# The identity of a delta-rule solve's first level, moved from VectorE to GpSimd, one tile behind another

## The chip, the cores and the metric

The kernel runs on one core of a Trainium2 chip, as one program of 69,816 instructions. The metric is the device time of one execution in microseconds (us). Five engines work side by side, each through its own list of instructions in order: TensorE (PE), VectorE (DVE), ScalarE (ACT), GpSimd (POOL) and SyncE (SP, which here starts transfers). They wait for each other through semaphores.

## The reference, cut to what matters

The reference is one inference step of a decoder layer: two feed-forward blocks, attention, and an RWKV-7 time mixing whose core is a delta-rule recurrence over a matrix state of each head:

```python
def step(S, inp):
    rt, wt, kt, vt, at, bt = inp
    sa = jnp.einsum("bhvk,bhk->bhv", S, at)
    S = S * wt[:, :, None, :] + sa[..., None] * bt[:, :, None, :] + vt[..., None] * kt[:, :, None, :]
    return S, jnp.einsum("bhvk,bhk->bhv", S, rt)
```

There are 8 heads of 64, a prompt of 1024 tokens and 8 samples of 4 tokens (32 tokens). All is float32. Only the stage that computes this recurrence is changed.

## The kernel before

The stage is `rwkv_phase` (L2106 to L2800), and it lies between about 2050 and 2550 us of the span. The recurrence is cut into chunks of 32 tokens (4 for the samples). Inside a chunk the dependence of each token on the earlier ones is a triangular system, which is solved by doubling: the inverse of 2x2 blocks first, then `LEVELS` = 4 levels, each of which joins blocks of twice the size.

**Tiles and groups.** A tile is 128 tokens of one pair of heads. There are 9 tiles for each of 4 pairs of heads: 8 of prompt and one of samples. Three tiles make a group i (0 to 11), which is tiles 3i to 3i+2. The third tile of groups 2, 5, 8 and 11 is the sample tile, and its expansions are 8 chunks wide where the others are 4. The text calls groups by what the group after them is: the elementwise work "ahead" is done for group i+1 while group i is solved, and it is 384 tokens wide, but 288 where group i+1 holds the samples (i = 1, 4, 7, 10).

**One written-out order.** A list `jobs` (L2224 to L2229) fixes the order of all work. Every engine walks the same list and does its own part of each job, in that order. For each group the list has:
- `start_of(i)`: for the three tiles `turn` (four transposes, copied out by ACT), `products` for two halves (PE; DVE masks the results into `prod` and `xx`, L2603 and L2605), `seed` (adds the identity to `xx`, L2527), then for each level `off` (PE; DVE out L2608) and `grow` (PE; DVE out L2613), then `nv` and `gh`;
- merged evenly into it, `chain_of(i-1)`: the recurrence from chunk to chunk of the group before (`chain`, PE L2786, DVE out L2636; `y`, L2663 and L2645);
- merged evenly into that, `spread_of(i)` (POOL) and `beside`, which is `ahead_of(i+1)` and `after_of(i-2)`;
- at the end `rest_of(i)`: `rgy`, `trans`, `add`.

**Jobs that matter here.** `spread` is the job "expansions": POOL builds `b_exp` and `k_exp` (L2402) and `decay` (L2410) of one tile. They are needed by `trans` and `add` at the end of the group. `mix_k` (DVE: difference L2515, mix L2518, scale L2538), `mix_r` (L2515, L2518) and `mix_v` (POOL: difference L2373; DVE: mix L2518) form the inputs of group i+1. `scan` is a prefix sum on DVE (L2542), after which POOL does two subtractions (L2360, L2363). `w`, `a` and `g` (L2675, L2677, L2679) and `norm`, `rksum`, `mean`, `var` (all L2693) are single wide products of PE. PE's results go through 7 PSUM banks in turn: a job may start when the job 7 places earlier in PE's list has been read out.

**Waits of the seed.** `off` of level 0 waits for `seeded` (L2720). `mix_v` on DVE waits for POOL's difference through `v_diffed` (L2516).

Of the kernel before, what the change touches and what calls it, by code (L numbers as in the profile page):

```python
# [10 lines left out]
ALU = mybir.AluOpType  # L11
# [3 lines left out]
P = 128  # L15
# [2090 lines left out]
def rwkv_phase(nc, env, masks, lw, lg, proj, shift, params, lora_w, not_start, state_in, yb_dram,  # L2106
# [10 lines left out]
    LEVELS, GT, BANKS, HB = 4, 3, 7, P // 2  # L2117
# [5 lines left out]
    with Phase(nc) as ctx:  # L2123
        def sb(n, shape):
            return ctx.enter_context(nc.sbuf_tensor(f"rw_{n}", shape, F32))

        def sem(n):
            return ctx.enter_context(nc.semaphore(f"rw_{n}"))
# [14 lines left out]
        xx = sb("xx", [P, GT, 4, HB])  # L2143
# [12 lines left out]
        expanded, seeded, decayed, rg_done = (sem(n) for n in ("expanded", "seeded", "decayed", "rg_done"))  # L2156
# [12 lines left out]
        strict4, level_mask, chunk_mask, seeds, ident_half = masks  # L2169

        def halves(t):
            return 1 if t % NTILE == NTILE - 1 else 2
# [7 lines left out]
        def tiles_of(i):  # L2180
            return range(i * GT, (i + 1) * GT)

        def start_of(i):
            g = tiles_of(i)
            first = [("turn", t, 0) for t in g]
            first += [("products", t, h) for t in g for h in range(2)]
            first += [("seed", t, 0) for t in g]
            for lv in range(LEVELS):
                first += [("off", t, lv) for t in g] + [("grow", t, lv) for t in g]
            return first + [("nv", t, 0) for t in g] + [("gh", t, 0) for t in g]  # L2190

        def rest_of(i):
            g = tiles_of(i)
            rest = [("rgy", t, a) for t in g for a in range(halves(t))]
            return rest + [("trans", t, 0) for t in g] + [("add", t, 0) for t in g]
# [18 lines left out]
        def spread_of(i):  # L2214
            return [("spread", t, 0) for t in tiles_of(i)]

        def merged(x, more):

            out = []
            for n, item in enumerate(x):  # L2220
                out += [item] + more[n * len(more) // len(x):(n + 1) * len(more) // len(x)]
            return out

        jobs = ahead_of(0)  # L2224
        for i in range(NI):
            beside = merged(ahead_of(i + 1), after_of(i - 2)) if i + 1 < NI else after_of(i - 2)
            now = merged(start_of(i), chain_of(i - 1)) if i else start_of(i)
            jobs += merged(now, spread_of(i) + beside) + rest_of(i)
        jobs += merged(chain_of(NI - 1), after_of(NI - 2)) + after_of(NI - 1)  # L2229

        NO_PE = ("mix_k", "scan", "sq", "mix_r", "exp", "mix_v", "root", "kp", "kt", "ar_r", "kn", "ar_a", "ysq",
# [15 lines left out]
        def wait_out(eng, job):  # L2247

            eng.wait_ge(out_by[job], emptied[job])
# [4 lines left out]
        def own(t):  # L2254
            return t % GT
# [89 lines left out]
        @block.gpsimd  # L2345
        def _(pool):
            pool.memset(padded[:, 0, :, 0:1], 0.0).then_inc(zeroed, 1)
            pool.memset(ar[:, GT - 1, GT - 1, :, T_DEC:], 0.0).then_inc(zeroed, 1)
            for x in (bt, kt, bh, kh, v):
                pool.memset(x[:, GT - 1, SAMPLE + T_DEC:], 0.0).then_inc(zeroed, 1)  # L2350
            pool.memset(s_none[:, :], 0.0).then_inc(zeroed, 1)
            pool.memset(seeds[:, 0, :], 0.0).then_inc(zeroed, 1)
            pool.wait_ge(zeroed, 9)
            pool.tensor_copy(seeds[:, 0, 0:HB:2], ident_half[:, 1:HB:2]).then_inc(zeroed, 1)
            for kind, i, _ in jobs:
                if kind == "scan":
                    _, g, w, _ = place(i)
                    pool.wait_ge(scanned, i + 1)
                    wait(pool, bh_done, i)
                    pool.tensor_tensor(sg[:, 0:w], cum[:, 0:w], sg[:, 0:w], ALU.subtract)  # L2360
                    for lo, hi, c in [(0, GC, CHUNK)] if g < GT - 1 else [(0, SAMPLE, CHUNK), (SAMPLE, w, DEC_SEQ)]:
                        x = cum[:, lo:hi].rearrange("p (n t) -> p n t", t=c)
                        ins = pool.tensor_tensor(to_end[:, lo:hi].rearrange("p (n t) -> p n t", t=c),  # L2363
                                                 x[:, :, c - 1:c].broadcast_to([P, (hi - lo) // c, c]), x,
                                                 ALU.subtract)
                    ins.then_inc(ended, 1)
                elif kind == "mix_v":
                    p, g, _, _ = place(i)
                    pool.wait_ge(loaded[g], LOADS[g] * (p + 1))
                    if i >= GT:  # L2370
                        wait_out(pool, ("rksum", i - GT, 0))
                    for cur, prev, out in pieces(g, 2, v[:, g, :]):
                        pool.tensor_tensor(out, prev, cur, ALU.subtract).then_inc(v_diffed, 1)  # L2373
                elif kind == "kt":
                    _, g, w, _ = place(i)
                    pool.wait_ge(kp_done, i + 1)
                    pool.wait_ge(exped, i + 1)
                    pool.tensor_tensor(kh[:, g, 0:w], k[:, 0:w], to_end[:, 0:w], ALU.mult).then_inc(kh_done, 1)
                elif kind == "ar_a":
                    _, g, w, _ = place(i)  # L2380
                    pool.wait_ge(bb_done, i + 1)
                    pool.tensor_tensor(bh[:, g, 0:w], a_in[:, 0:w], to_end[:, 0:w], ALU.mult).then_inc(bh_done, 1)
                elif kind == "ygate":
                    p, _, w, _ = place(i)
                    x = y[:, i % 2, 0:w]
                    pool.wait_ge(y_scaled, i + 1)
                    pool.tensor_scalar(x, x, par[:, p, PAR_LNW:PAR_LNW + 1], par[:, p, PAR_LNB:PAR_LNB + 1],
                                       ALU.mult, ALU.add).then_inc(affine, 1)
                    pool.wait_ge(affine, i + 1)
                    wait_out(pool, ("rksum", i, 0))  # L2390
                    pool.tensor_tensor(x, x, bonus[:, i % 4, 0:w], ALU.add).then_inc(with_bonus, 1)
                    pool.wait_ge(with_bonus, i + 1)
                    wait_out(pool, ("g", i, 0))
                    pool.tensor_tensor(x, x, g_out[:, i % 4, 0:w], ALU.mult).then_inc(gated, 1)
                elif kind == "spread":
                    t, o, n = i, own(i), chunks(i)
                    wait_out(pool, ("turn", t, 0))
                    if t >= GT:
                        wait_done(pool, ("add", t - GT, 0))
                    m = chunk_mask(t)  # L2400
                    for dst, col in ((b_exp, 2), (k_exp, 3)):
                        pool.tensor_tensor(dst[:, 4 * o:4 * o + n, :],  # L2402
                                           tok[:, o, col:col + 1, :].broadcast_to([P, n, P]),
                                           m.rearrange("p (n a) -> p n a", a=1).broadcast_to([P, n, P]),
                                           ALU.mult).then_inc(expanded, 1)
                    if t >= GT:
                        wait_out(pool, ("trans", t - GT, 0))
                    pool.wait_ge(exped, t // GT + 1)
                    c0 = 4 * o
                    pool.tensor_tensor(decay[:, 4 * o:4 * o + n, :],  # L2410
                                       ident_half.rearrange("p (a n) -> p a n", a=1).broadcast_to([P, n, 64]),
                                       e_c[:, slot(t), c0:c0 + n].rearrange("p (n a) -> p n a", a=1)
                                       .broadcast_to([P, n, 64]), ALU.mult).then_inc(decayed, 1)
# [92 lines left out]
        def _(dve):  # L2506
# [14 lines left out]
            for job in jobs:  # L2521
                kind, i, a = job
                if kind == "seed":

                    o = own(i)
                    wait_out(dve, ("products", i, 1))
                    dve.tensor_tensor(xx[:, o, :, :], xx[:, o, :, :],  # L2527
                                      ident_half.rearrange("p (a n) -> p a n", a=1).broadcast_to([P, 4, HB]),
                                      ALU.add).then_inc(seeded, 1)
                    continue  # L2530
                if kind in NO_PE:
                    p, g, w, cols = place(i)
# [48 lines left out]
                if kind in ("norm", "rksum", "mean"):  # L2581
                    _, g, w, _ = place(i)
# [14 lines left out]
                t, o, lt = i, own(i), i % NTILE  # L2597
                i = t // GT
# [22 lines left out]
                elif kind == "trans":  # L2621
                    n = chunks(t)
# [400 lines left out]
```

## Time and profile before

| | |
|---|---|
| median of 3 runs | 3797.13 us (3793.44 to 3805.70) |
| the profiled execution, its own time | 3798.92 us |
| its span in the profile | 3797.1 us |
| its mean granted TensorE clock | 0.944 of full speed |
| busy over the span: PE, DVE, ACT, POOL | 90%, 44%, 25%, 11% |
| from 2090 to 2540 us: PE, DVE, ACT, POOL busy | 386.8, 333.8, 160.8, 185.9 us of 450 |

A row of a timeline gives start and length in us, engine, line, operation, what is written and read, and how often in a row; in brackets stands the idle time of the engine before it, and what ended it. The ends of matmuls are modelled and overlap, so on PE the distance between starts says more than the length. DVE and POOL instructions overlap their neighbours by some hundredths too.

### The profile page before, as it was taken

Reading aid. Unit: us, or ns where it says so; the run is one execution under the profiler, and the core shown is the slowest. Engines: PE = TensorE matmul, PEld = TensorE weight load, DVE = VectorE, ACT = ScalarE, POOL = GpSimd, SP = SyncE. Lnnn points to the kernel's source line nnn. Section 1 sums busy time; section 2 is a strip of 40 time slices with the busy share of each in tenths; the row PEclk is TensorE's granted clock in tenths of the full one; section 3 lists DMA queues with packets and bytes.
Section 4 is the critical chain, followed back from the end, with each engine's and each line's share of the span. In section 5 each row is a group of like instructions: output and inputs, shape, how many; then the busy total and the mean of one; then the engine's idle time right before and its main releaser. Section 6 shows DMA issues by size and latency. Waiting matters only on the chain. (4 is left out here: it accounts for less than half of the span.)

```text
span 3797.1 us, 69816 instructions
## 1 busy us (share of the span) xinstructions
PE 3436.2 (90%) x29021; PEld 3071.1 (81%) x29021; DVE 1678.9 (44%) x2939; ACT 935.5 (25%) x1619; POOL 428.2 (11%) x452
## 2 busy tenths in 40 slices
PE   7999999979999799979994888878979999999877
PEld 6999999978999646756663676768969999999866
DVE  3343343353222245435443777755243344344454
ACT  3111111121001104534442333324241111111231
POOL 0000000020000000033331444430010000000112
PEclk9999999989999898989996899989989999999988
DMA  2111111123222300056553010004131011011032
GB/s 104 35 55 45 40 50 45 40 78 115 90 90 90 123 2 13 9 190 206 195 201 86 14 32 25 16 32 175 35 130 50 35 52 49 34 52 47 24 139 99
DMA packets 118587, 279.27 MB, mean 74 GB/s; under 512 B 45876, under 2 KB 56948, under 8 KB 117780
## 3 DMA queue, kind: packets, MB, share of 16 engines
q1 hardware_dynamic: 99892, 199.87, 15.7%
q0 software_dynamic: 18432, 75.51, 5.8%
q8 instruction: 212, 3.47, 0.4%
q14 instruction: 51, 0.42, 0.0%
HBM read 231.41 MB, written 43.80 MB: 72 GB/s over the span
## 5 line engine op out<-in xcount | busy, mean ns | idle before, releaser
L79 PE MATMUL f_psg<-f_u_hi,f_w_hi 128*128 128x352 f32 x1056 | 348.7, 330 | 46.1 <-DVE f_u_lo L359 23.0
L590 DVE TENSOR_TENSOR c_x<-c_x,f_psd 128x352 f32<-128x352 f32 x480 | 246.2, 519 | 317.0 <-PE f_psd L81 317.0
L79 PE MATMUL f_psd<-f_hid_hi,f_w_hi 128*128 128x352 f32 x1056 | 349.8, 331 | 18.2 <-DVE c_x L590 9.8
L475 ACT ACTIVATE f_w_hi<-f_raw 128x1024 fp32r<-128x1024 f32 x132 | 136.8, 1054 | 912.6 <-PE f_psd L81 352.0
L80 PE MATMUL f_psg<-f_u_lo,f_w_hi 128*128 128x352 f32 x1056 | 343.5, 325 | 0.0
L81 PE MATMUL f_psg<-f_u_hi,f_w_lo 128*128 128x352 f32 x1056 | 343.4, 325 | 0.0
L79 PE MATMUL f_psu<-f_u_hi,f_w_hi 128*128 128x352 f32 x1056 | 341.6, 323 | 0.4 <-DVE f_w_lo L479 0.4
L80 PE MATMUL f_psd<-f_hid_lo,f_w_hi 128*128 128x352 f32 x1056 | 341.3, 323 | 0.0
L81 PE MATMUL f_psd<-f_hid_hi,f_w_lo 128*128 128x352 f32 x1056 | 340.9, 323 | 0.0
L80 PE MATMUL f_psu<-f_u_lo,f_w_hi 128*128 128x352 f32 x1056 | 339.1, 321 | 0.0
L81 PE MATMUL f_psu<-f_u_hi,f_w_lo 128*128 128x352 f32 x1056 | 338.7, 321 | 0.0
L479 DVE TENSOR_TENSOR f_w_lo<-f_raw,f_w_hi 128x1024 fp32r<-128x1024 f32 x132 | 161.6, 1238 | 361.2 <-ACT f_w_hi L475 361.2
L79 PE MATMUL in_ps<-in_u_hi,inw_hi 128*128 128x352 f32 x864 | 284.3, 329 | 12.3 <-DVE in_u_lo L359 8.9
L81 PE MATMUL in_ps<-in_u_hi,inw_lo 128*128 128x352 f32 x864 | 282.0, 326 | 0.0
L80 PE MATMUL in_ps<-in_u_lo,inw_hi 128*128 128x352 f32 x864 | 280.5, 325 | 0.0
L79 PEld LDWEIGHTS f_psg<-f_u_hi,f_w_hi 128*128 128x128 f32 x1056 | 202.4, 192 | 58.2 <-DVE f_u_lo L359 30.0
L118 POOL TENSOR_TENSOR n_total<-n_total,n_sq 128x1056 f32<-128x1056 f32 x18 | 44.5, 2470 | 1687.4 <-ACT n_sq L111 1687.4
L79 PEld LDWEIGHTS f_psd<-f_hid_hi,f_w_hi 128*128 128x128 f32 x1056 | 199.3, 189 | 35.0 <-DVE c_x L590 20.2
L80 PEld LDWEIGHTS f_psg<-f_u_lo,f_w_hi 128*128 128x128 f32 x1056 | 202.9, 192 | 0.0
L81 PEld LDWEIGHTS f_psg<-f_u_hi,f_w_lo 128*128 128x128 f32 x1056 | 202.2, 192 | 0.0
L80 PEld LDWEIGHTS f_psd<-f_hid_lo,f_w_hi 128*128 128x128 f32 x1056 | 199.7, 189 | 0.0
L81 PEld LDWEIGHTS f_psd<-f_hid_hi,f_w_lo 128*128 128x128 f32 x1056 | 199.6, 189 | 0.0
(403 smaller groups left out, 7178.6 us busy)
## 6 DMA issues: line engine op xcount, KB each, us to landing
f_raw<-in_ffn_gu SPq DMA_DIRECT2D x88, 512.0 KB, 4.2
f_raw<-in_ffn_d SPq DMA_DIRECT2D x44, 512.0 KB, 3.8
proj<-in_out SPq DMA_DIRECT2D x36, 528.0 KB, 2.9
inw_raw<-in_w_in_units SPq DMA_DIRECT2D x36, 512.0 KB, 3.9
h<-c_x SPq DMA_DIRECT2D x24, 528.0 KB, 2.9
c_x<-proj SPq DMA_DIRECT2D x16, 528.0 KB, 4.3
mgw_raw<-in_merge_units SPq DMA_DIRECT2D x16, 512.0 KB, 4.6
plw_raw<-in_ple_units SPq DMA_DIRECT2D x8, 640.0 KB, 3.9
```

The source lines that it names most:

```text
L79: pe.matmul(out, w_hi, x_hi, start=start, stop=False)
L80: pe.matmul(out, w_hi, x_lo, start=False, stop=False)
L81: return pe.matmul(out, w_lo, x_hi, start=False, stop=stop)
L118: eng.tensor_tensor(total, total, self.buf.sq[:, c % 2, :], ALU.add).then_inc(self.added, 1)
L475: act.activation(w_hi[:, u % 3, :], raw[:, u % 3, :], ACT.Copy).then_inc(hi_done, 1)
L479: dve.tensor_tensor(w_lo[:, u % 3, :], raw[:, u % 3, :], w_hi[:, u % 3, :], ALU.subtract).then_inc(lo_done, 1)
L590: dve.tensor_tensor(a, a, ps_d[:, n % 2, 0:TB], ALU.add).then_inc(added, 1)
```

## The change

The identity is added by POOL, and the list of jobs is put in another order. The three `seed` jobs no longer follow all six `products` jobs: each stands behind its own tile's. The three `spread` jobs, which were merged in at the front of the group, now follow the third `seed` in `start_of(i)`, and are no longer in the list that is merged in beside. As the lists are merged by their lengths, the jobs of `beside` also shift against those of `start_of` and `chain_of`.

```diff
             first = [("turn", t, 0) for t in g]
-            first += [("products", t, h) for t in g for h in range(2)]
-            first += [("seed", t, 0) for t in g]
+            for t in g:
+                first += [("products", t, 0), ("products", t, 1), ("seed", t, 0)]
+            first += spread_of(i)
...
-            jobs += merged(now, spread_of(i) + beside) + rest_of(i)
+            jobs += merged(now, beside) + rest_of(i)
...
+                elif kind == "seed":
+                    o = own(i)
+                    wait_out(pool, ("products", i, 1))
+                    pool.tensor_tensor(xx[:, o, :, :], xx[:, o, :, :],
+                                       ident_half.rearrange("p (a n) -> p a n", a=1).broadcast_to([P, 4, HB]),
+                                       ALU.add).then_inc(seeded, 1)
...
                 if kind == "seed":
-
-                    o = own(i)
-                    wait_out(dve, ("products", i, 1))
-                    dve.tensor_tensor(xx[:, o, :, :], xx[:, o, :, :],
-                                      ident_half.rearrange("p (a n) -> p a n", a=1).broadcast_to([P, 4, HB]),
-                                      ALU.add).then_inc(seeded, 1)
                     continue
```

For group 5 the list up to `mix_v` reads as follows (capitals: jobs of `beside`; a number after a dot is a half, a level or a chunk).

Before: turn15 turn16 turn17 **spread15** chain12.0 products15.0 **spread16** products15.1 products16.0 **spread17** chain12.1 products16.1 W products17.0 products17.1 A chain12.2 **seed15 seed16** MIX_K **seed17** chain12.3 MEAN off15.0 off16.0 SCAN y12 off17.0 G grow15.0 grow16.0 SQ chain13.0 grow17.0 off15.1 YSQ off16.1 chain13.1 MIX_R off17.1 grow15.1 NORM grow16.1 chain13.2 EXP grow17.1 off15.2 VAR off16.2 chain13.3 off17.2 MIX_V

After: turn15 turn16 turn17 W chain12.0 products15.0 products15.1 A **seed15** chain12.1 MIX_K products16.0 products16.1 **seed16** MEAN chain12.2 products17.0 products17.1 SCAN **seed17** chain12.3 G **spread15 spread16 spread17** SQ y12 off15.0 YSQ off16.0 off17.0 chain13.0 MIX_R grow15.0 grow16.0 grow17.0 NORM chain13.1 off15.1 EXP off16.1 off17.1 chain13.2 VAR grow15.1 grow16.1 MIX_V grow17.1 chain13.3 off15.2 ROOT off16.2 off17.2

## Rows read from the trace of the kernel before

**Rows 1.** Who waited for whom, 2090 to 2540 us: total, times, longest.
```profile
PE rw_ps L2725 <- DVE rw_s L2636: 15.2, 8, 2.6
PE rw_ps L2725 <- DVE rw_xx L2527: 14.4, 16, 2.4
```

**Rows 2.** Groups of DVE instructions, 2090 to 2540 us: busy us, mean ns, idle before.
```profile
L2527 DVE TENSOR_TENSOR rw_xx<-rw_xx,c_ident_half 128x256 f32<-128x256 f32 x36 | 36.6, 1048 | 0.0
...
L2542 DVE TENSOR_TENSOR_SCAN rw_cum<-rw_starts,rw_sg 128x384 f32<-128x384 f32 x7 | 6.6, 945 | 0.0
...
L2518 DVE SCALAR_TENSOR_TENSOR rw_r<-rw_r,rw_par,rw_padded 128x384 f32<-128x384 f32 x7 | 4.3, 619 | 0.2
...
L2515 DVE TENSOR_TENSOR rw_r<-rw_padded 128x384 f32<-128x384 f32 x7 | 3.8, 547 | 0.0
L2538 DVE TENSOR_SCALAR rw_kk<-rw_k,rw_par 128x384 f32<-128x384 f32 x7 | 2.9, 420 | 0.2
```

**Rows 3.** Timeline of POOL, group 5 (its third tile's expansions).
```profile
2280.35 1.90 POOL L2402 TENSOR_TENSOR rw_b_exp<-rw_tok,c_in_chunk 128x1024 f32<-128x1024 f32 x1
...
2284.24 1.22 POOL L2410 TENSOR_TENSOR rw_decay<-c_ident_half,rw_e_c 128x512 f32<-128x512 f32 x1
```

**Rows 4.** Timeline of DVE, group 5.
```profile
2279.18 0.43 DVE L2603 TENSOR_TENSOR rw_prod<-rw_ps,c_strict 128x256 f32<-128x256 f32 x1 [0.48 <-PE rw_ps L2716]
...
2279.71 0.41 DVE L2603 TENSOR_TENSOR rw_prod<-rw_ps,c_strict 128x256 f32<-128x256 f32 x1
...
2280.59 3.96 DVE L2527 TENSOR_TENSOR rw_xx<-rw_xx,c_ident_half 128x256 f32<-128x256 f32 x2
2284.48 1.39 DVE L2515 TENSOR_TENSOR rw_k<-rw_padded 128x384 f32<-128x384 f32 x1
...
2298.07 0.61 DVE L2518 SCALAR_TENSOR_TENSOR rw_v<-rw_v,rw_par,rw_padded 128x384 f32<-128x384 f32 x1
```

**Rows 5.** Timeline of PE, group 5: first transpose, chain12.0, w, off17.0, off17.2.
```profile
2273.85 0.33 PE L2706 MATMUL rw_ps<-c_ident,rw_ar 128*128 128x128 f32 x1
...
2275.31 0.33 PE L2786 MATMUL rw_ps<-rw_s,rw_trans 64*64 64x64 f32 x4
...
2277.52 0.91 PE L2675 MATMUL rw_ps<-c_lw,rw_lora 64*128 64x384 f32 x2
...
2287.47 0.69 PE L2725 MATMUL rw_ps<-rw_xx,rw_prod 64*64 64x64 f32 x8 [1.91 <-DVE rw_s L2636]
...
2297.42 0.40 PE L2725 MATMUL rw_ps<-rw_xx,rw_prod 64*64 64x64 f32 x8
```

**Rows 6.** Busy us by stretch: PE, PEld, DVE, ACT, POOL, then PEclk, DMA, GB/s.
```profile
2284.00:2292.00 8.00, 5.39 (x74) 4.12 (x76) 6.22 (x14) 2.21 (x4) 4.03 (x5) 0.57 0.00 0
```

**Rows 7.** Groups of POOL instructions, 2090 to 2540 us.
```profile
L2402 POOL TENSOR_TENSOR rw_k_exp<-rw_tok,c_in_chunk 128x512 f32<-128x512 f32 x32 | 34.7, 1084 | 0.0
...
L2410 POOL TENSOR_TENSOR rw_decay<-c_ident_half,rw_e_c 128x256 f32<-128x256 f32 x32 | 21.4, 669 | 0.0
...
L2360 POOL TENSOR_TENSOR rw_sg<-rw_cum,rw_sg 128x384 f32<-128x384 f32 x7 | 7.0, 994 | 24.2 <-DVE rw_cum L2542 24.2
...
L2363 POOL TENSOR_TENSOR rw_to_end<-rw_cum 128x384 f32<-128x384 f32 x7 | 5.8, 825 | 0.0
L2373 POOL TENSOR_TENSOR rw_v<-rw_padded 128x384 f32<-128x384 f32 x7 | 5.8, 824 | 0.0
```

**Rows 8.** Timelines, groups 4 and 6: first transpose, and DVE's part of mix_v.
```profile
2238.81 0.33 PE L2706 MATMUL rw_ps<-c_ident,rw_ar 128*128 128x128 f32 x1
...
2259.98 0.64 DVE L2518 SCALAR_TENSOR_TENSOR rw_v<-rw_v,rw_par,rw_padded 128x256 f32<-128x256 f32 x2
...
2314.52 0.33 PE L2706 MATMUL rw_ps<-c_ident,rw_ar 128*128 128x128 f32 x1
...
2335.95 0.61 DVE L2518 SCALAR_TENSOR_TENSOR rw_v<-rw_v,rw_par,rw_padded 128x384 f32<-128x384 f32 x1
```

**Rows 9.** Timeline of DVE, group 11: its three seeds.
```profile
2508.28 4.93 DVE L2527 TENSOR_TENSOR rw_xx<-rw_xx,c_ident_half 128x256 f32<-128x256 f32 x3
```

## The prediction

> **What bounds the kernel now.** I read the page first: the change touches one stage, about 450 of 3797 us, in which PE is busy 387 us and DVE 334 us. So neither engine is idle for long, and what counts is where each group of three tiles loses time. The list of waits names the place [rows 1]: at `off` of level 0 PE waited 14.4 us for seeds and 15.2 us for a copy of `chain` that stands behind the seeds on DVE. The two together, 29.6 us over 12 groups, are what could be won directly. The groups of DVE instructions say why the seeds are late [rows 2]: 36 of them take 36.6 us, 1048 ns each, although they are no larger than the masking of the products, which takes 0.41 us [rows 4]. The timelines of group 5 show what stretches them. The two seeds at 2280.59 last 3.96 us, about 2 us each, just while POOL does the expansions of the sample tile from 2280.35 [rows 3, 4]. The difference of `mix_k` behind them takes 1.39 us [rows 4] where the same difference for `mix_r`, with POOL idle, takes 0.55 us [rows 2]. The masking of the products, which reads one side from PSUM, ran at 0.41 to 0.43 us beside POOL's work too [rows 4]. PE then stands still (1.91 us before off17.0 alone [rows 5]), and its granted clock falls: 0.57 as a mean from 2284 to 2292, which is mostly the lower of its two levels, 1.2 GHz [rows 6].
>
> The Trainium skill, "SBUF — State Buffer", section "Who interferes with whom", has a rule for this: a DVE instruction with two SBUF inputs and a GpSimd instruction that reads SBUF lock each other out for a whole instruction. By that rule a seed behind a 2 us expansion lasts 2 us, which is what the trace shows (3.96 us for two). The same rule speaks against the change as well: seeds on GpSimd can be held up by DVE's two-input instructions, here `mix_k` and `scan`, by up to the 0.5 to 0.95 us that these last.
>
> **The change part by part.** Times are from the group's first transpose (T). I follow the two lists of the text above, for a group with 384 columns ahead.
>
> *Removed from DVE:* three seeds, 3 x 1.05 = 3.1 us a group [rows 2], and the stretching of `mix_k`, about 0.8 us (1.39 against 0.55). In group 5 that is nearly the whole hole of PE before off17.0.
>
> *The seed on POOL:* the trace has no such instruction. The nearest rows are `decay`, the same 256 columns, two inputs, at 669 ns, and the 384 column differences at 824 to 994 ns [rows 7]. From below it can't be under DVE's unstretched 0.41, and from above 0.99. I take 0.65, from the row of equal size.
>
> *The order on POOL, which is the heart of it.* The list of after puts `scan` in front of the third seed. POOL goes through it in order, so the third seed waits for DVE's scan and then for POOL's own two subtractions. When is the scan done?
> - The turns end at T+1.46 (2273.85 to 2275.31). Six jobs of chain and products followed in 2.21 us, so 0.37 each [rows 5]. After has turns, w, chain, 2 products, a, chain: 1.46 + 2 x 0.91 + 4 x 0.37 = T+4.8.
> - DVE copies that chain (0.2), does `mix_k` unstretched (0.55 + 0.62 + 0.42 = 1.6 [rows 2]), two products (0.53 apart, from 2279.18 and 2279.71 [rows 4], 1.06), the mean (about 0.5, the size of the 384 column rows), a chain (0.15), two products (1.06) and the scan (0.95): T+10.3.
> - POOL: 0.99 + 0.83 [rows 7], then the seed 0.65: T+12.7. Without the scan ahead of it the third seed would be done at about T+10.0.
>
> So off of the third tile starts at T+12.8. Before it started at T+13.6 in group 5 (2287.47), with `g` still to come. PE gains there, some 2 to 3 us in group 5 and under 1 us where no sample tile stretched the seeds.
>
> *The expansions.* They follow the third seed, where before they followed the turns (T+1.5). Three tiles take 3 x (2 x 1.08 + 0.67) = 8.5 us by the mean rows [rows 7], less some overlap, 8.3; with a sample tile two of 2.65 and one of 5.1 (2280.35 to 2284.24 + 1.22 [rows 3]), with 0.4 for DVE in between 10.8. They end at T+21.0 and T+23.5. Their own users, `trans` and `add`, come later than that, so that is hidden. But behind them on POOL stands the difference of `mix_v`, 0.83 [rows 7], and DVE waits for it **at a place that the new list has moved forward**: before grow17.1, not behind off17.2. DVE's mix ends 0.6 later:
> - 384 ahead, no samples: T+22.4. Before it ended at 2336.5, T+22.0 [rows 8], and with four more copies done, which I put at 0.2 each, so after stands at 23.2: **1.3 us later**.
> - 288 ahead: the narrower w, a, mix_k, scan and subtractions bring the third seed 0.9 us forward, T+11.8, expansions to 20.1, differences and mix 1.4: T+21.5, with a grow, a chain and three offs to copy, 1.1: 22.6. Before: 2260.6, T+21.8 [rows 8]. **0.85 later**.
> - With the sample tile: 23.5 + 0.83 + 0.6 = T+24.9, with 1.1: 26.0. Before: 2298.7, T+24.8 [rows 4, 5]. **1.25 later**.
>
> What waits behind: DVE's copy of the third grow of level 1, and through it the third off of level 2, on which PE stops once it has done the few jobs ahead of it. PE's own lag, by the same sum in group 5, is off17.2 at 24.9 + 0.35 = T+25.3 against 2297.42, T+23.6: 1.7 us [rows 5]. From there on DVE is nearly always busy until the end of the group, so what is late there stays late.
>
> *The last group* has nothing ahead, so neither the scan nor mix_v. Its seeds take DVE 4.93 us before [rows 9]; on POOL the third follows its products within 0.7, so about 3.5 us are won.
>
> *The granted clock.* DVE arrives at mix_v at about T+20.5 and stands there 1 to 4 us, longest with the sample tile. A hole of that size before off17.0 dropped PE's clock to the lower level [rows 5, 6]. I add 1 us for each of three groups; the bounds are nothing and the 3 us or so that PE's 5.39 us of work in such a stretch [rows 6] lost.
>
> *The sum:* 4 x 1.3 + 4 x 0.85 + 3 x 1.25 = 12.4, less 3.5, plus 3: **+12 us**. By PE's lag in place of DVE's it is 11 x 1.7 - 3.5 + 3 = +18; with the seed at its bounds (-0.25, +0.35) 11 groups give -3 and +4. The profiled execution took 3798.9 us, 1.8 over the median; applied to the median of 3797.1 it gives **3809 us**.
>
> **The rivals.**
> - *POOL is done in time, and the win stays.* If POOL is through the expansions before DVE gets to mix_v, the stall goes, and what counts is the earlier end of level 0. In group 5, with PE at its full clock, I make that about 3 us; 0.7 us in the eight others; 3.5 in the last group: 3 x 3 + 8 x 0.7 + 3.5 = -18 us, 3779. It decides if the difference of `mix_v` is out by about T+20.5, and by my sum it is out at 21.8. For it speaks the size of the waits [rows 1]; against it, that 8.3 us of POOL work have moved by some 11 us. A partial form, the expansions 1 us earlier than my sum in each group, ends at about 0.
> - *The two cancel.* The early gain is kept as slack that PE uses up while DVE waits: PE has four or five jobs of 0.3 to 0.45 us to do before it needs the missing copy, and its idle places later in the group soak up 1 us of the lag. Then 11 x 0.3 + 3 - 3.5, within 5 us of before.
> - *The stall costs more.* PE's clock falls at each stall, and `mix_r` (two instructions with both inputs in SBUF), now beside the expansions, is stretched as `mix_k` was, by 0.8 us: 11 x (1.7 + 0.8) + 3 = +30 us, 3827.
> - *The third seed itself is the new hole*, 2.3 us of idle PE before off17.0. It is in my sum, but hidden under the later stall. Alone it ends near before.
>
> **How the numbers follow.** About 0.3% (11 us) is what a measurement of this kernel can tell from no change. My forecast (+4 to +20) has 0.45, costs more 0.1, cancel 0.25, the win stays (with its partial forms) 0.2. Half or more of my own case lies above 11 us: slower 0.45 of it and the dear case together come to 0.48, the same 0.3, faster 0.22. The range leaves out the outer parts of the first and third rival: 3784 to 3825.
>
> **What would show it.** Right: no wait of PE for the seeds of the first two tiles; DVE's seeds gone and the difference of mix_k at 0.55 us; POOL's third seed directly behind L2363; a wait of DVE at L2518 for POOL's `rw_v` L2373 of 1 to 4 us in most groups, which before had almost none; a PE wait for `rw_xx` L2613 behind it. Wrong: if that wait is absent, the first rival has it; if it is there and the stage is no longer than before, the second. Most of all I could be wrong in the 1 us by which two sums of twelve terms differ.

## The result and the profile after

The changed kernel takes 3820.69 us (median of 6 runs, 3815.61 to 3825.72), the one before 3804.34 us in the same session (6 runs, 3793.44 to 3806.25). The medians are 16.4 us apart. The ratio that is used here and below isn't that of the medians: it is 1.0049, with a 95% interval of 1.0038 to 1.0060, which makes the changed kernel slower by 19 us (14 to 23). The prediction was +12 us. The profiled execution took 3817.18 us, with a span of 3815.4 us and a mean granted clock of 0.944, as before.

First, who waited for whom in the changed kernel, 2090 to 2570 us (total us, times, longest). It answers to [rows 1].

```profile
PE rw_ps L2726 <- POOL rw_xx L2399: 24.3, 12, 4.9
PE rw_ps L2787 <- DVE rw_s L2637: 22.0, 22, 2.6
...
DVE rw_v L2525 <- POOL rw_v L2374: 10.3, 6, 3.0
PE rw_ps L2726 <- DVE rw_s L2637: 10.3, 6, 3.5
```

PE's wait for DVE's seeds is gone and a longer one for POOL's third seed stands in its place: 24.3 us against 14.4. DVE's wait for `rw_v`, which the prediction was built on, is there, but in 6 groups of 11, and only in four of them (0, 2, 5 and 8) for 1 us or more. The second row is new too: at `chain` PE waits 22.0 us for DVE's copies, where in the kernel before it waited 12.1 (2090 to 2540 us):

```profile
PE rw_ps L2786 <- DVE rw_s L2636: 12.1, 15, 2.3
```

Next the groups of instructions that answer to [rows 2] (busy us, mean ns, idle before).

```profile
L2399 POOL TENSOR_TENSOR rw_xx<-rw_xx,c_ident_half 128x256 f32<-128x256 f32 x36 | 26.9, 746 | 118.2 <-DVE rw_xx L2606 117.3 <-PE rw_ps L2726 0.9
...
L2522 DVE TENSOR_TENSOR rw_r<-rw_padded 128x384 f32<-128x384 f32 x7 | 7.4, 1064 | 0.0
L2525 DVE SCALAR_TENSOR_TENSOR rw_r<-rw_r,rw_par,rw_padded 128x384 f32<-128x384 f32 x7 | 7.2, 1033 | 0.2
L2522 DVE TENSOR_TENSOR rw_k<-rw_padded 128x384 f32<-128x384 f32 x7 | 5.7, 820 | 0.0
```

`mix_r` takes 1064 + 1033 ns where before it took 547 + 619 [rows 2]: it now lies beside the expansions. The timeline of POOL in group 5 (T = 2288.45) shows the order in which they come.

```profile
2296.43 0.72 POOL L2399 TENSOR_TENSOR rw_xx<-rw_xx,c_ident_half 128x256 f32<-128x256 f32 x1 [2.67 <-DVE rw_xx L2606]
2298.94 1.00 POOL L2361 TENSOR_TENSOR rw_sg<-rw_cum,rw_sg 128x384 f32<-128x384 f32 x1 [1.79 <-DVE rw_cum L2543]
2299.90 0.82 POOL L2364 TENSOR_TENSOR rw_to_end<-rw_cum 128x384 f32<-128x384 f32 x1
2300.68 0.72 POOL L2399 TENSOR_TENSOR rw_xx<-rw_xx,c_ident_half 128x256 f32<-128x256 f32 x1
2301.36 1.04 POOL L2409 TENSOR_TENSOR rw_b_exp<-rw_tok,c_in_chunk 128x512 f32<-128x512 f32 x1
...
2310.84 1.04 POOL L2417 TENSOR_TENSOR rw_decay<-c_ident_half,rw_e_c 128x512 f32<-128x512 f32 x1
2311.84 0.82 POOL L2374 TENSOR_TENSOR rw_v<-rw_padded 128x384 f32<-128x384 f32 x1
```

The third seed stands behind the scan's two subtractions and ends at 2301.40, T+12.95. The difference of `mix_v` stands behind all expansions and ends at T+24.2. What PE and DVE do about it in the same group:

```profile
2301.55 0.69 PE L2726 MATMUL rw_ps<-rw_xx,rw_prod 64*64 64x64 f32 x8 [2.56 <-POOL rw_xx L2399]
...
2313.86 0.69 PE L2726 MATMUL rw_ps<-rw_xx,rw_prod 64*64 64x64 f32 x8 [2.87 <-DVE rw_s L2637]
```

```profile
2302.63 1.18 DVE L2522 TENSOR_TENSOR rw_r<-rw_padded 128x384 f32<-128x384 f32 x1
2303.85 0.85 DVE L2525 SCALAR_TENSOR_TENSOR rw_r<-rw_r,rw_par,rw_padded 128x384 f32<-128x384 f32 x1
...
2312.77 0.62 DVE L2525 SCALAR_TENSOR_TENSOR rw_v<-rw_v,rw_par,rw_padded 128x384 f32<-128x384 f32 x1 [2.37 <-POOL rw_v L2374]
```

PE stands still twice, 2.56 us for the third seed and 2.87 us for off17.2, where before the longest of the group was 1.91 us [rows 5]. The clock is at the lower level when PE resumes after the first (0.50 from 2300 us on) and falls again after the second (busy us of PE, PEld, DVE, ACT, POOL, then PEclk, DMA share, GB/s):

```profile
2302.00:2305.00 3.00, 3.00 (x61) 3.00 (x58) 2.69 (x6) 0.80 (x2) 3.00 (x4) 0.50 0.00 0
2312.00:2317.00 5.00, 3.14 (x63) 3.17 (x65) 3.61 (x11) 0.00 (x0) 1.57 (x2) 0.66 0.02 3
```

From 2302 to 2305 PE works without a pause at 0.50, the 1.2 GHz level. The same view for the whole of group 5, in the kernel before and in the changed one:

```profile
2273.85:2314.52 40.67, 33.64 (x711) 27.18 (x707) 30.75 (x82) 14.26 (x33) 18.13 (x17) 0.92 0.16 25
2288.45:2331.32 42.87, 34.49 (x711) 28.21 (x707) 26.99 (x79) 14.21 (x33) 20.49 (x20) 0.88 0.16 26
```

PE does the same number of matmul instructions in both, 711, but is busy 0.85 us longer, at a mean clock of 0.88 instead of 0.92.

In the groups with 288 columns ahead DVE hardly waits for `rw_v`. Group 4 (T = 2251.83), timeline of DVE:

```profile
2265.28 1.56 DVE L2522 TENSOR_TENSOR rw_r<-rw_padded 128x256 f32<-128x256 f32 x2
2266.88 2.14 DVE L2525 SCALAR_TENSOR_TENSOR rw_r<-rw_r,rw_par,rw_padded 128x256 f32<-128x256 f32 x2
...
2273.23 0.64 DVE L2525 SCALAR_TENSOR_TENSOR rw_v<-rw_v,rw_par,rw_padded 128x256 f32<-128x256 f32 x2
```

`mix_r` takes 3.70 us there (1.56 + 2.14), and DVE comes to `mix_v` only when POOL's difference is ready. In the kernel before the same two rows are:

```profile
2255.47 0.51 DVE L2515 TENSOR_TENSOR rw_r<-rw_padded 128x256 f32<-128x256 f32 x2
2256.02 0.65 DVE L2518 SCALAR_TENSOR_TENSOR rw_r<-rw_r,rw_par,rw_padded 128x256 f32<-128x256 f32 x2
```

**Where the time went.** From first transpose to first transpose, groups 0 to 10 took 412.4 us before and 431.5 after: +19.1. By kind: +4.8 over the four plain groups (0, 3, 6, 9), +7.7 over the four with 288 columns ahead, +6.5 over the three with the sample tile. From the last group's first transpose (2502.32 and 2525.78) to the stage's last POOL instruction (its end at 2554.95 and 2573.57) it is 52.6 and 47.8: -4.8. So the stage is 14.2 us longer. The first transposes are another 4.4 us apart, in code that the change doesn't touch, and that is within chance: in the traces of the ten experiments, whose code up to there is the same, the first transpose lies between 2088.07 and 2100.03 us. Of the 19.1 us, PE stands idle for 15.5 and is busy 3.6 longer (355.4 and 359.0 us).

### The profile page after: what moved, and what is told of

It reads as the page before. It is cut to its first block and busy times, and to the rows that moved or that the text cites. A ratio compares the mean times of both kernels' runs of the same rounds, so it can differ in the third digit from the quotient of the medians.

```text
span 3815.4 us, 69816 instructions
## 1 busy us (share of the span) xinstructions
PE 3437.9 (90%) x29021; PEld 3070.7 (80%) x29021; DVE 1656.7 (43%) x2903; ACT 935.1 (25%) x1619; POOL 453.8 (12%) x488
## 5 line engine op out<-in xcount | busy, mean ns | idle before, releaser
L79 PEld LDWEIGHTS f_psu<-f_u_hi,f_w_hi 128*128 128x128 f32 x1056 | 199.2, 189 | 0.8 <-DVE f_w_lo L479 0.8
```

Of the source, the lines that this page charges most:

```text
L79: pe.matmul(out, w_hi, x_hi, start=start, stop=False)
```

## The experiments

Each was run beside the kernel before, whose median was 3799.6, 3800.7 and 3800.3 us in the three sessions; "back" is against the changed kernel's 1.0049. The 95% interval stands behind each ratio; it is 3 to 7 us to either side, so differences of 1 to 3 us between versions are not resolved. Most alter only the order in which one engine walks the list. POOL then walks `order` in place of `jobs`, and DVE, ACT and PE keep theirs:

```python
order = list(jobs)
def behind(job, at):
    if job in order and order.index(job) < order.index(at):
        order.remove(job)
        order.insert(order.index(at) + 1, job)
def ahead(job, at):
    if job in order and order.index(job) > order.index(at):
        order.remove(job)
        order.insert(order.index(at), job)
```

It adds 14 to 17 lines, so L2399 of the changed kernel is L2413 to L2416 there.

**Scan's subtractions behind the third seed**

```diff
+            for n in range(NI):
+                behind(("scan", n + 1, 0), ("seed", n * GT + 2, 0))
```

> POOL alone walks the changed list with its two subtractions of the scan behind the third seed instead of ahead of it. Theory (the wait of DVE at mix_v for POOL's difference decides, as in the prediction): the third seed comes about 2 us sooner, but the difference of mix_v is as late as before, so most of what is won at the seed is given back there: at most 8 us of the 19 us come back, 3812 to 3819 on the scale where before is 3804. Rival (the hole before the third off of level 0 decides; the list of waits of the changed kernel has 24.3 us there and only 10.3 us at mix_v): 15 to 22 us come back, at or under the time of before, 3798 to 3806.

3819.44 us, ratio 1.0047 (1.0031 to 1.0064): 1 us back, which is nothing. Its waits:

```profile
DVE rw_v L2539 <- POOL rw_v L2388: 28.9, 11, 5.1
PE rw_ps L2740 <- DVE rw_s L2651: 25.1, 6, 5.6
...
PE rw_ps L2740 <- POOL rw_xx L2413: 6.8, 9, 2.9
```

PE's wait for POOL's seeds falls from 24.3 to 6.8 us, and DVE's for `rw_v` grows from 10.3 to 28.9. The early seed was won and paid back at `mix_v`: while POOL's difference is late, the third seed is hidden under it.

**POOL's difference of mix_v ahead of the expansions**

```diff
+                ahead(("mix_v", n + 1, 0), ("spread", n * GT, 0))
```

> POOL alone walks the changed list with the difference of mix_v ahead of the three expansions instead of behind them. Theory (mix_v decides): the 10.3 us of DVE waits go, and PE's waits and low clock behind them: 10 to 18 us come back, 3803 to 3811 where before is 3804. Rival (the third seed decides): under 6 us come back, 3815 or more.

3805.07 us, ratio 1.0014 (1.0001 to 1.0027): 13 us back of 19. DVE no longer waits for `rw_v`; in group 5 its mix ends at T+21.8 (2306.50 against 2284.74). By kind of group, in its trace, the three sample groups win 9.3 us (119.1 against 128.4), the four plain ones 2.6, and the four with 288 columns ahead only 0.8 (145.7 against 146.5, and 138.8 in the kernel before). The wait for the third seed is untouched:

```profile
PE rw_ps L2740 <- POOL rw_xx L2413: 25.4, 13, 4.9
```

**Both moves.** The two lines of the two runs above together.

> Both moves on POOL: third seed, two subtractions, difference of mix_v, then the expansions. If the two waits hide each other, as the prediction has it, the two together give more than the sum of the single ones, and the kernel is faster than before by what the prediction's first rival worked out: 3780 to 3794 where before is 3804. If the loss sits in the order of the jobs on PE and DVE and not in POOL's order, it stays at 3810 or more.

3793.68 us, ratio 0.9987 (0.9974 to 1.0000): 24 us back, where the two alone gave 1 and 13. So with `mix_v` out of the way the third seed is worth another 11 us. That is 5 us faster than before, where 10 to 24 were expected. In its trace the 288-column groups are now back at 139.2 us, so what they had lost came back only with the third seed. What may hold the rest back is in its groups of instructions:

```profile
L2569 DVE SCALAR_TENSOR_TENSOR rw_k<-rw_gate,rw_k 128x384 f32<-128x384 f32 x7 | 9.2, 1316 | 0.2
L2540 DVE SCALAR_TENSOR_TENSOR rw_r<-rw_r,rw_par,rw_padded 128x384 f32<-128x384 f32 x7 | 8.3, 1186 | 0.2
```

`rw_k<-rw_gate` took 559 ns in the kernel before, where no expansion lay beside it. The expansions have been moved onto other steps of DVE.

**The new order alone, seeds on DVE.** 

```diff
-                elif kind == "seed":
...
                 if kind == "seed":
+                    o = own(i)
+                    wait_out(dve, ("products", i, 1))
+                    dve.tensor_tensor(xx[:, o, :, :], xx[:, o, :, :],
...
```

> The changed list, with the seeds left on DVE: the order without the change of engine. The seeds then take DVE 3 x 0.35 us a group and do not wait behind the scan's two subtractions on POOL. Theory (mix_v decides): the expansions start where they did in the changed kernel less 0.7 us, mix_v is still late, 3812 to 3820. Rival (the third seed decides): 3798 to 3808.

3814.64 us, ratio 1.0048 (1.0031 to 1.0066): the whole loss, a little above the 8 to 16 us expected, without any seed on POOL. The seeds are no longer stretched on DVE (451 ns against 1048), and it doesn't help:

```profile
L2527 DVE TENSOR_TENSOR rw_xx<-rw_xx,c_ident_half 128x256 f32<-128x256 f32 x36 | 16.2, 451 | 0.7
...
DVE rw_v L2519 <- POOL rw_v L2374: 25.4, 11, 5.1
```

**The engine alone, old order.** 

```diff
-            for t in g:
-                first += [("products", t, 0), ("products", t, 1), ("seed", t, 0)]
-            first += spread_of(i)
+            first += [("products", t, h) for t in g for h in range(2)]
+            first += [("seed", t, 0) for t in g]
...
-            jobs += merged(now, beside) + rest_of(i)
+            jobs += merged(now, spread_of(i) + beside) + rest_of(i)
```

> The list of before, seeds on POOL: the change of engine without the new order. On POOL the seeds stand behind the three expansions. By the rows of before these end 8.4 us after the first transpose (11.6 with a sample tile), and the seeds follow, 0.7 us each. Theory: PE waits for them about as long as it waited for the stretched seeds of before, mix_k on DVE is still stretched, and mix_v is not touched: within 8 us of before, 3793 to 3809 where before is 3800. Rival (the engine is what costs): slower by 12 us or more.

3809.59 us, ratio 1.0023 (1.0012 to 1.0034): 9 us slower than before, just outside the 8 of the theory and below the 12 of the rival. What the trace shows is not what costs in the changed kernel: POOL now has the expansions ahead of all three seeds, and DVE's `mix_k` lies beside their end (waits, and groups):

```profile
PE rw_ps L2725 <- POOL rw_xx L2398: 41.8, 19, 4.7
```

```profile
L2524 DVE SCALAR_TENSOR_TENSOR rw_k<-rw_k,rw_par,rw_padded 128x384 f32<-128x384 f32 x7 | 10.9, 1551 | 0.2
L2521 DVE TENSOR_TENSOR rw_k<-rw_padded 128x384 f32<-128x384 f32 x7 | 8.9, 1275 | 0.0
L2538 DVE TENSOR_SCALAR rw_kk<-rw_k,rw_par 128x384 f32<-128x384 f32 x7 | 6.9, 986 | 0.2
```

**The kernel before, POOL's expansions behind its difference of mix_v.** DVE does the seeds and the list is the old one; POOL alone walks it in another order.

```diff
+            for n in range(NI):
+                for t in reversed(range(n * GT, n * GT + GT)):
+                    behind(("spread", t, 0), ("mix_v", n + 1, 0) if n + 1 < NI else ("seed", n * GT + 2, 0))
```

> The list of before on all engines, seeds on DVE; POOL alone does the three expansions behind the difference of mix_v. Theory: seeds (1.05 us) and mix_k's difference (1.3) fall to 0.45 and 0.55 us, nothing waits for POOL, the collision moves to later DVE instructions with two SBUF inputs, where it costs a part: 3786 to 3796 where before is 3800. Rival (stretched seeds are hidden anyway): within 3 us of before.

3796.89 us, ratio 0.9991 (0.9982 to 1.0000), about 3 us won and less than expected. Against the kernel before, the seeds fall from 1048 to 524 ns, which frees DVE of 19.0 us (36.6 - 17.6). `rw_k<-rw_gate` rises to 1460 ns, `rw_rk` to 1067, `rw_gate` to 1141 and the mix of `mix_r` to 1277:

```profile
L2542 DVE TENSOR_TENSOR rw_xx<-rw_xx,c_ident_half 128x256 f32<-128x256 f32 x36 | 17.6, 524 | 0.0
...
L2568 DVE SCALAR_TENSOR_TENSOR rw_k<-rw_gate,rw_k 128x384 f32<-128x384 f32 x7 | 10.2, 1460 | 0.2
...
L2565 DVE TENSOR_SCALAR rw_gate<-rw_a_in,rw_par 128x384 f32<-128x384 f32 x7 | 8.0, 1141 | 0.0
```

**Both moves, seeds on DVE.** The two lines of both moves and the edit that puts the addition back in DVE's part.

> As e3_both (changed list, POOL: two subtractions, difference of mix_v, then expansions), but with the seeds on DVE. It tells what the engine is worth once the order on POOL is mended: POOL's seed is 0.73 us and leaves DVE 0.35 us free. Theory (engine hardly matters): within 4 us of e3_both. Rival (DVE bound): 8 us slower than e3_both or more.

3798.18 us, ratio 0.9995 (0.9984 to 1.0005). With the seeds on POOL it was 0.9987, 3 us less, and the two intervals overlap: with this order on POOL, the engine of the seeds makes no difference that these runs can tell.

**Both moves, and the first tile's expansions ahead of the first seed**

```diff
+                ahead(("spread", n * GT, 0), ("seed", n * GT, 0))
```

> As e3_both, with the first tile's expansions ahead of the first seed on POOL, in the 3 us in which POOL stood idle. The other two then end 2.6 us sooner, and kp on DVE (1.32 us instead of 0.56 in e3_both) is stretched less. If the collisions are what is left, 3 to 8 us faster than e3_both; if the first seed is now late, no gain or a loss.

3782.44 us (5 runs, 3779.43 to 3785.92), ratio 0.9957 (0.9944 to 0.9971): 16 us faster than before, 11 faster than both moves alone (3 to 8 were expected), and the fastest of all. In the changed kernel POOL stood idle for 7.03 us ahead of the first seed of group 5; here it does one tile's expansions there (T = 2271.76):

```profile
2273.13 1.04 POOL L2425 TENSOR_TENSOR rw_b_exp<-rw_tok,c_in_chunk 128x512 f32<-128x512 f32 x1 [3.81 <-ACT rw_tok L2526]
2274.12 1.04 POOL L2425 TENSOR_TENSOR rw_k_exp<-rw_tok,c_in_chunk 128x512 f32<-128x512 f32 x1
2275.12 0.61 POOL L2433 TENSOR_TENSOR rw_decay<-c_ident_half,rw_e_c 128x256 f32<-128x256 f32 x1
2276.34 0.73 POOL L2415 TENSOR_TENSOR rw_xx<-rw_xx,c_ident_half 128x256 f32<-128x256 f32 x1 [0.60 <-DVE rw_xx L2622]
```

The seed isn't delayed (it still waits for DVE). DVE is idle until 2274.44 and then copies a chain and masks products out of PSUM, which isn't stretched (0.42 and 0.28 us). `rw_k<-rw_gate` is back at 559 ns. But POOL is also done with the group's expansions 3 us sooner (T+21.7 in group 5, T+24.7 with both moves alone), and no run tells how much of the 11 us is due to either.

**DVE's part of mix_v back at its old place.** The changed kernel; only DVE's walk of the list differs.

```diff
-            for job in jobs:
+            order = list(jobs)
+            for n in range(NI - 1):
+                late, at = ("mix_v", n + 1, 0), ("off", n * GT + 2, 2)
+                if order.index(late) < order.index(at):
+                    order.remove(late)
+                    order.insert(order.index(at) + 1, late)
+            for job in order:
```

> The changed kernel, but DVE alone does its part of mix_v where the kernel before has it, behind the eviction of the third tile's second level; POOL's order is untouched (third seed, third expansions, then its difference for mix_v). Theory (what costs is that DVE's step is brought forward past the point where POOL's difference is ready): no waits of DVE for rw_v from POOL, 8 to 14 us of the changed kernel's 19 us come back, like putting POOL's difference first did; the wait of PE for the third seed (24 us in 12 places) stays. 1.5 to 3 us slower per 1000 less: ratio to before 1.001 to 1.003. Rival (DVE's place does not matter, the stretches of DVE's steps beside POOL or the third seed's wait make the whole loss): ratio stays at 1.004 to 1.006.

3815.27 us, ratio 1.0041 (1.0028 to 1.0055): the rival holds. (Its profiled execution, 3804.69 us, was its quickest, so its trace serves for the order of things and not for lengths.) DVE's wait shrinks to 4.0 us, but `rw_v` is no sooner done:

```profile
2303.13 0.62 DVE L2525 SCALAR_TENSOR_TENSOR rw_v<-rw_v,rw_par,rw_padded 128x384 f32<-128x384 f32 x1 [0.80 <-POOL rw_v L2374]
```

The mix ends at T+24.9 (2303.75 against 2278.81), as in the changed kernel. What costs here is when POOL's difference is ready, not where DVE asks for it.

**The second tile's expansions early as well**

```diff
+                ahead(("spread", n * GT + 1, 0), ("seed", n * GT + 1, 0))
```

> The version with both POOL moves and the first tile's expansions ahead of the first seed, and now the second tile's expansions ahead of the second seed as well, in POOL's pause of about 2.7 us between the seeds. Theory (POOL's expansions cost only where DVE's shared steps lie beside them or where a seed comes late): if they fit the pause, 0 to 8 us faster than without it (ratio to before 0.9935 to 0.9957). Rival (they delay the second seed or stretch DVE's mix_k in front of it, and PE waits for the second tile): slower than without it by 3 to 12 us (ratio 0.9965 to 0.999).

3803.56 us, ratio 0.9999 (0.9986 to 1.0012): by the ratios 16 us slower than with one tile early, more than the 3 to 12 of the rival. (Its profiled execution, 3810.00 us, was its slowest.) POOL's pause between the first two seeds was 2.66 us long, and DVE's `mix_k` lies in it. Timeline of DVE, then of POOL, group 5 (T = 2284.70):

```profile
2290.46 1.28 DVE L2542 SCALAR_TENSOR_TENSOR rw_k<-rw_k,rw_par,rw_padded 128x384 f32<-128x384 f32 x1
2291.78 1.08 DVE L2556 TENSOR_SCALAR rw_kk<-rw_k,rw_par 128x384 f32<-128x384 f32 x1
```

```profile
2292.60 0.72 POOL L2434 TENSOR_TENSOR rw_decay<-c_ident_half,rw_e_c 128x256 f32<-128x256 f32 x1
2293.99 0.72 POOL L2416 TENSOR_TENSOR rw_xx<-rw_xx,c_ident_half 128x256 f32<-128x256 f32 x1 [0.67 <-DVE rw_xx L2623]
```

Two steps of `mix_k` took 2.36 us instead of 1.04 (0.62 + 0.42, as with one tile early), the copy of a chain and the second tile's products behind them came late, and PE's waits at `chain` for DVE's copies rose from 21.2 to 35.0 us (22 places).

## Why the prediction was right, and where its sizes were off

The sign, the cause and 12 of 19 us came out; four terms of the sum were off. In the traces the stage is 14.2 us longer, against a sum of 11.9, and part of that closeness is luck: 4.3 us too little for the 288-column groups stand against 0.4, 0.25 and 1.3 too much for the others. The prediction's second sum, by PE's lag of 1.7 us a group, has 18.7 for the 11 groups, which measured 19.1; it added the clock to that once more.

- **The order on POOL.** Right almost to the tenth in the sample groups. In group 5 the third seed ends at T+12.95 (12.7 predicted), POOL's difference of `mix_v` at T+24.2 and DVE's mix at T+24.9 (24.9), off17.2 starts at T+25.4 (25.3). In groups 3, 6 and 9 the seed and the difference are 0.7 us later than predicted (T+13.4 and T+22.5, for 12.7 and 21.8). DVE comes to `mix_v` at T+21.95 in group 5, not at T+20.5, so its wait is 2.4 us. That the lateness of `mix_v` is the larger part of the loss is shown: moving POOL's difference alone gave 13 us back, moving the seed alone nothing, both 24. By kind of group that holds for the sample groups, where it gave 9.3 us back, and not for the 288-column ones.
- **"At a place that the new list has moved forward"** was the half of the argument that did not matter. With the place moved back, the loss stayed within the interval.
- **"The third seed itself is the new hole"**, called hidden under the later stall: shown by the first three experiments. PE's wait for it is the longest of the stage's new waits (24.3 us), yet it is worth 1 us while `mix_v` is late, and 11 once it isn't. In the traces its gain falls in the 288-column groups (145.7 to 139.2 us) and in the plain ones (153.9 to 147.6), not in the sample groups (119.1 to 120.1). The list of waits alone would have named the wrong one.
- **Mis-sized: the 288-column groups.** 4 x 0.85 = 3.4 us were put down, 7.7 measured. DVE's `mix_v` ended at T+22.0 and not T+21.5, and in groups 4, 7 and 10 for another reason than forecast: there is no wait for POOL left, as `mix_r` beside the expansions takes 3.70 us instead of 1.16 and DVE comes late. The stretching of `mix_r` had been left to the rival "the stall costs more", at 0.8; in 384-column groups it measured 0.93 (1064 + 1033 - 547 - 619 ns), in group 4 2.5. That mechanism belonged into the sum. So did the third seed's hole, 2.3 us of PE in groups 4 and 7, which moving `mix_v` alone left as it was, with 6.9 of the 7.7 us. The clock isn't separated from the two: from the kernel before to the changed one its mean fell from 0.95 to 0.91 in groups 4, 7 and 10, but rose from 0.90 to 0.95 in group 1, which lost as much (2.2 us). The stretching may also be why a wait of 1 to 4 us for `rw_v`, forecast for most groups, was found in four: in group 4, read above, DVE was held up before it got there.
- **Mis-sized, plain groups.** 4 x 1.3 = 5.2 predicted, 4.8 measured, but by two errors: three groups lost 1.5 to 2.4 us, and group 9 became 0.9 shorter, because it had been 2.5 us longer than its like in the kernel before (39.9 against 37.5 and 37.4 for groups 3 and 6). There its mean clock was 0.87, that of the two others 0.95, and PE was busy 35.4 us against 33.0 and 32.9 with the same jobs, so the clock made group 9 longer there; why it was low isn't shown.
- **Sample groups:** 3.75 and 3 for the clock, 6.75 in all, against 6.5 measured. The two low stretches of group 5 agree with it. With the same instructions PE is busy 3.3 us longer over the three groups (104.2 against 100.9) and idle 3.2 longer, so by these rows, whose ends of matmuls are modelled, about half of the 6.5 is the clock, as forecast.
- **The last group:** -3.5 predicted, -4.8 measured; with the new order and the seeds left on DVE it is -4.3 (48.3 us), so it is mostly the order that wins it and not the engine.
- **What would show it.** No wait of PE for the first two tiles' seeds: one of 0.44 us is left, in group 0. The wait of PE behind DVE's stall was named as one for `rw_xx`; that has 4.0 us, and the larger part, 10.3 us, is put down to the copy of a chain (`rw_s`) that stands behind the same step.
- **Small prices.** The seed on POOL took 0.75 us where 0.65 was taken from the row of equal size, inside its bounds. "The difference of `mix_k` at 0.55 us" failed: 0.82, as POOL's first seed starts beside it. What that cost isn't shown.

The sum of the dear rival, +30, leaves out the 3.5 us of the last group that the other sums take off; with them it is +27.

Two things stay open: how the ratio's 19 us (14 to 23) and the 14.2 of the two traces go together, and the part played by the other jobs of the merged list, which shifted too. PE's waits at `chain` for DVE's copies are a sign of it: 12.1 us before, 22.0 in the changed kernel, and still 21.3 to 21.5 with POOL's difference moved and with both moves, but 5.6 with the old list and the seeds on POOL. In the run with the old place of `mix_v`, DVE does `rw_gate` and `rw_k` ahead of the copies of the second level; the kernel before has them behind. No run isolates that.

The Trainium skill, "SBUF — State Buffer", section "Who interferes with whom", says that the engine that issues second is shut out for the whole of the other's instruction, and counts among what can collide not only two-input instructions but also a `tensor_scalar` with its quick two-port form. The traces agree on both: 1551 against 619 ns for a two-input mix and 986 against 420 ns for the scale of `mix_k`, in the run with the engine alone changed. That the scale runs in its quick form fits its 420 ns, where a two-input difference of the same 384 columns takes 547.

## What to carry to other kernels

An engine that takes over a short step takes it at its own place in its own queue: work out for each job behind it when it now comes out, and look for the user with the earliest need, not for the longest wait. In these runs the expansions on GpSimd stretched the VectorE steps with their inputs in SBUF beside them, wherever they were put. Moving them won most where GpSimd was idle and VectorE idle too or reading PSUM, as ahead of the first seed (-11 us for one tile, and +16 for a second one in a pause that looked long enough). Where two waits lie one behind the other, undo each alone and both together: 1, 13 and 24 us here. And add up the time by kind of group: the total hides that one of the two cost mostly in the sample groups and the other in the rest.

## What the runs showed of the hardware

- One VectorE step can lose more than its own length beside GpSimd: two-input steps of 0.55 to 0.62 us took 2.07 and 2.13 us in group 5 of the run with only the engine changed, as long as the 1.90 and 2.21 us expansions beside them.

```profile
2287.94 2.07 DVE L2521 TENSOR_TENSOR rw_k<-rw_padded 128x384 f32<-128x384 f32 x1
2290.04 2.13 DVE L2524 SCALAR_TENSOR_TENSOR rw_k<-rw_k,rw_par,rw_padded 128x384 f32<-128x384 f32 x1
```

- The stretching goes both ways: on POOL the addition took 0.72 us alone and 1.31 us beside VectorE's scan (0.94 us), in the fastest version:

```profile
2281.39 1.31 POOL L2415 TENSOR_TENSOR rw_xx<-rw_xx,c_ident_half 128x256 f32<-128x256 f32 x1 [0.93 <-DVE rw_xx L2622]
```
